# Query weights stored in the order in which they are loaded: runs of 16 KB per partition in place of 2 KB

## The reference

```python
def peer(h, w_query, sub_keys, expert_u, expert_v):      # h: 256 x 2048, in blocks of 128 tokens
    def block(xb):
        q = (xb @ w_query).reshape(128, 8, 2, 128)       # w_query: 2048 x 2048, 16.8 MB
        s = jnp.einsum('thpd,hpnd->thpn', q, sub_keys)   # scores against 2 x 128 keys for each head
        sv, si = lax.top_k(s, 16)
        ...                                              # 16 x 16 candidates, their best 16
        gate = jax.nn.softmax(top_s)
        act = jax.nn.gelu(jnp.einsum('thkd,td->thk', expert_u[idx], xb))
        return jnp.einsum('thk,thkd->td', gate * act, expert_v[idx])
```

## Time and profile before

| what | value |
|---|---|
| median of three runs | 1866.18 us |
| the profiled execution, device time | 1864.87 us |
| its span in the trace | 1863.2 us |
| PE busy | 1593.6 us (86%) |
| DVE busy | 1050.5 us (56%) |
| DMA packets, bytes | 73442, 724.64 MB, mean 389 GB/s |
| queue q0 (POOL) | 53472 packets, 613.75 MB, 78.8% of 16 engines |
| queue q1 (SP) | 17264 packets, 107.30 MB, 14.1% of 16 engines |

### The profile page before, as it was taken

The page is one execution under the profiler, slowest core; times in us unless marked ns, Lnnn a source line. Parts: engine busy times, 40 slices in busy tenths (PEclk is TensorE's granted clock), DMA queues, the critical chain, the costliest instruction groups (busy, mean ns, idle before and its releaser), DMA issues. The chain is left out here.

```text
span 1863.2 us, 13323 instructions
## 1 busy us (share of the span) xinstructions
PE 1593.6 (86%) x4518; PEld 761.0 (41%) x4518; DVE 1050.5 (56%) x1706; ACT 397.9 (21%) x1168; POOL 438.0 (24%) x384
## 2 busy tenths in 40 slices
PE   6999999999999979999877886877759687687776
PEld 2355445565458854443333332333324233232332
DVE  2237775675558873433546556465665656646445
ACT  2121013222010023222212222221223212122112
POOL 0000000001005565556322222221213122121212
PEclk9999999999999989999999999999889898999999
DMA  9998866548978999999999999999999999999997
GB/s 401 427 376 351 336 256 247 214 186 348 421 276 346 418 422 422 421 421 421 425 428 427 428 428 427 428 428 428 428 427 415 428 429 428 428 427 428 428 428 303
DMA packets 73442, 724.64 MB, mean 389 GB/s; under 512 B 7432, under 2 KB 9816, under 8 KB 20000
## 3 DMA queue, kind: packets, MB, share of 16 engines
q0 software_dynamic: 53472, 613.75, 78.8%
q1 hardware_dynamic: 17264, 107.30, 14.1%
q10 hardware_dynamic: 2640, 2.75, 0.5%
HBM read 721.63 MB, written 2.15 MB: 388 GB/s over the span
## 5 line engine op out<-in xcount | busy, mean ns | idle before, releaser
L1318 PE MATMUL ps<-ring,wg 128*128 128x512 f32 x1168 | 541.0, 613 | 130.5 <-ACT wg L851 111.0
L1766 DVE SCALAR_TENSOR_TENSOR ring<-ring,A 128x2048 f32<-128x2048 f32 x142 | 324.6, 2291 | 307.3 <-DMA ring<-in_expert_rows,acc 223.1
L1318 PEld LDWEIGHTS ps<-ring,wg 128*128 128x128 f32 x1168 | 221.8, 195 | 444.6 <-issue 275.8
L1023 PE MATMUL ps<-ring,H 128*128 128x512 f32 x512 | 222.1, 593 | 2.2 <-ACT rows_and_values L655 2.1
L513 POOL DMA_INDIRECT ring<-in_expert_rows,acc x106 | 116.1, 1095 | 388.7 <-PE ps L1318 376.5
L846 ACT ACTIVATE rows_and_values<-rows_and_values 128x1 f32<-128x1 f32 x256 | 50.9, 199 | 704.6 <-DVE ring L1766 398.4
L1318 PE MATMUL ps<-H,wg 128*128 128x512 f32 x360 | 167.3, 612 | 30.1 <-ACT wg L851 29.4
L1345 DVE SCALAR_TENSOR_TENSOR ring<-ring,rows_and_values 128x2048 f32<-128x2048 f32 x64 | 143.7, 2287 | 49.2 <-DMA ring<-in_mod_late 36.2
L1318 PE MATMUL ps<-rows_and_values,wg 128*128 128x512 f32 x288 | 135.5, 614 | 36.6 <-ACT wg L851 35.9
L1023 PEld LDWEIGHTS ps<-ring,H 128*128 128x128 f32 x512 | 96.4, 190 | 122.0 <-issue 118.9
L851 ACT ACTIVATE wg<-K,rows_and_values 128x128 f32<-128x128 f32 x256 | 102.7, 401 | 161.3 <-PE ps L1318 154.7
(11 more groups left out here) (281 smaller groups left out, 1464.4 us busy)
## 6 DMA issues: line engine op xcount, KB each, us to landing
ring<-in_mod_late POOLq DMA_DIRECT2D x32, 2048.0 KB, 10.5
ring<-in_mod_first SPq DMA_DIRECT2D x16, 2048.0 KB, 20.6
ring<-in_w_in SPq DMA_DIRECT2D x14, 2048.0 KB, 11.4
ring<-in_w_query SPq DMA_DIRECT2D x7, 2048.0 KB, 14.6
ring<-in_w_out SPq DMA_DIRECT2D x12, 1024.0 KB, 10.1
H<-in_tokens SPq DMA_DIRECT2D x4, 1024.0 KB, 13.0
queries_and_gates<-in_w_in SPq DMA_DIRECT2D x2, 1024.0 KB, 23.9
queries_and_gates<-neg_rows ACTq DMA_DIRECT2D x8, 256.0 KB, 5.2
```

Of the source, the lines that this page charges most:

```text
L1023: ins = mm(bank, H[:, kk, b * P:(b + 1) * P], W[kh][:, k, :], **flags)
L1318: ins = mm(ps[:, 4 * b + n, :], diag[:, r % 4, :], row[:, n * CH:(n + 1) * CH], start=k == 0, stop=r == BLOCK_RANKS - 1, skip_group_check= ...
L1766: v.scalar_tensor_tensor(out=rows_u, in0=rows_u, scalar=1.0, in1=A[:, r // BLOCK_RANKS, :], op0=ALU.mult, op1=ALU.mult, accum_out=dots[:, ...
```

## The change

The host lays out `w_query` with `pieces`, as it does `w_in` and `w_out`, so that its array is [4 blocks of columns, 2 halves, 128 partitions, 4096]. The two load functions read it in that shape. The bytes that land in each tile are the same, in the same places; the number, the order and the waits of the loads are the same. What differs is the run that lies together in HBM: 16 KB for each partition in a 2 MB piece (128 runs in place of 1024), and 8 KB in the two split pieces of 1 MB (128 in place of 512).

```diff
-        "w_out": pieces(w_out[0]), "w_query": w_query[0],
+        "w_out": pieces(w_out[0]), "w_query": pieces(w_query[0]),
...
             def load_third_query(kh, i, loaded):
-                k0 = (kh * KH + 4 * i) * P
-                sp.dma_start(WQ2[kh][i], w_query[k0:k0 + 4 * P, 2 * CH:3 * CH].rearrange(
-                    "(k p) n -> p k n", p=P)).then_inc(loaded, 16)
+                k0 = 4 * i * CH
+                sp.dma_start(WQ2[kh][i], w_query[2, kh, :, k0:k0 + 4 * CH].rearrange(
+                    "p (k n) -> p k n", k=4)).then_inc(loaded, 16)

             def load_query(n, kh):
                 base, loaded = (2, q_ld) if n % 2 == 0 else (0, w_ld)
-                sp.dma_start(W[base + kh], w_query[kh * KH * P:(kh + 1) * KH * P, n * CH:(n + 1) * CH
-                                                   ].rearrange("(k p) n -> p k n", p=P)).then_inc(loaded[kh], 16)
+                sp.dma_start(W[base + kh], w_query[n, kh].rearrange("p (k n) -> p k n", k=KH)
+                             ).then_inc(loaded[kh], 16)
```

## The result

The changed kernel took 1872.05 us, the median of seven runs (1870.87 to 1872.76), against 1866.18 for seven runs of the kernel before (1864.85 to 1866.84). The ratio is 1.0034, with a 95% interval of 1.0024 to 1.0043. The forecast was 1868.9, with a range up to 1871.4: the sign came out as worked out, the size did not, and a loss of over 0.2% had been given a chance of 0.28.

A forecast was written before the change was run, and what follows sets the result against it. DMA, filled by expert-row gathers from 700 to 1840 us, was taken as the bound. Row U 22 landing 2.7 us late gave 1864.87 + 2.7 = 1867.6 profiled, 1868.9 against the median 1866.18; 8-in-10 range 1864.4 to 1871.4.

The forecast's parts named there:

- Who gets the engines: Late query loads beside gathers: packets alternate one to one, so a 2 MB load takes 7.4 us in place of 25.
- part 2: Engine sharing at 578 to 682 us: long loads pass ahead of rows U, the third through at 618.0 us.
- The lateness of dot 15: Row U 15 late by 2.11 MB, 4.9 us, less 2 x 0.53 saved on two loads: 3.9 us.
- The empty DMA: During the pick of group 2, no query packets are left: DMA idle 3 to 5 us, near 636 to 640 us.
- My bounds: Landing of row U 22: 1.8 us late as U 0 on an empty DMA, 3.9 with 9.4 us again; 2.7 taken.
- the sum: Whole kernel: 1864.87 us profiled + 2.7 = 1867.6; against the median 1866.18, 1868.9.
- From U 22 to the end: Rows behind U 22 follow at the pace of the DMA; all 2.7 us reach V 0 and PE, nothing made up.
- The four slots starve: Rival before dot 15: more issues start under running dots, DMA empties, 2.1 us on top, 1871.0; chance 0.20.
- Sharing stays as it is: Rival: 16 KB runs served in smaller turns, dot 15 comes 1.1 us early, 1865.1 or 1864.6; chance 0.14.
- all of the saving counts: Rival: PE or the first gather hangs on the early loads, 4.3 us off, 1861.9; chance 0.05.
- The lateness is absorbed: Rival: part of the third load stays behind row U 15 and fills the lull, 1866.2 to 1867.5; chance 0.13.
- That a gain would be capped: At row V 0, issued behind PE's last scores: no more than 2.3 us can be gained.

The follow-up runs named there:

- late_2k: The changed kernel with the three query loads issued near 578, 595 and 609 us back in runs of 2 KB; 0.9995 of the kernel before.
- padded_2k: The changed kernel's layout with a gap of 256 bytes behind each 2 KB, so each packet is 2 KB again; 0.9999 of the kernel before.
- first_2k: The changed kernel with only the first late query load (near 578 us) back in runs of 2 KB; 1.0027 of the kernel before.
- late_16k: The kernel before with only the three late query loads in runs of 16 KB, the five early pieces in 2 KB; 1.0025 of it.
- second_16k: The changed kernel with the first and third late query loads back in 2 KB, only the middle one in 16 KB; 1.0014 of the kernel before.
- wait_dot15: The changed kernel with the last two query loads (n = 3) issued only after dot 15; 1.002 of the kernel before.
- third_16k: The changed kernel with the first two late query loads back in 2 KB, only the last (near 609 us) in 16 KB; 1.0005 of the kernel before.
- short_late: The kernel before with the three late query loads bringing only 128 of their 1024 rows, 5.5 MB left out; 0.9995 of it.
- third_waits: The changed kernel with only the last query load (n = 3, kh = 0) issued after dot 15; 1.0015 of the kernel before.

## Why the prediction was wrong in size, step by step

**Who gets the engines: right.** The packets alternate also at 16 KB (108 to 103 in 599 to 605 us). The third load was through at 620.9 us, 11.8 us after its issue: part 2 worked out 9.5 (2.1 + 7.4), but its first packet came 3.4 us after the issue in place of 2.1, and it moved for 8.4 us. It was still ahead of row U 15. late_2k and padded_2k show that neither the early loads nor the place in HBM takes part.

**The lateness of dot 15: 3.9 us worked out, 6.25 measured. This is the first step that failed.** The 2.11 MB that now come ahead are 5.0 us at 425 GB/s, as worked out. What was wrong is the term that I took off, 1.06 us saved on the first two loads. Counted from the empty DMA at 556 us to the same place behind dot 0, the kernel before (556 to 617.3 us) and the changed one (556 to 617.92 us) had moved:

```profile
DMA packets 4382, 21.08 MB, mean 344 GB/s; under 512 B 278, under 2 KB 278, under 8 KB 2322
```

```profile
DMA packets 2442, 20.95 MB, mean 338 GB/s; under 512 B 256, under 2 KB 256, under 8 KB 256
```

So nothing was won by then, and 0.13 MB, 0.3 us, were lost: what the longer packets saved went into the DMA left partly empty at 592 to 598 us, where the four slots starve (first_2k fills this stretch again). In late_16k, which has the same three long loads, the stretch is full (416 GB/s) and dot 15 is 4.97 us late, so not every execution pays this part. By the bytes row U 15 is then 3.9 + 1.06 + 0.3 = 5.3 us late.

The last 1.0 us is in how the row lands. The trace keeps sixteen landings for each transfer, which I take for one of each DMA engine, and the dot waits for the last of them. In the kernel before they came at 617.58 to 617.93 us, in the changed one at 623.03 to 624.81; their middle (617.69 and 623.48 us) is 5.2 us late behind dot 0, as the bytes have it, and the last 6.3. That the engines drift apart does not come from long packets: the sixteen landings of this row are 1.9 us apart in late_2k and 2.3 in padded_2k, and under 1.1 only in the kernel before and in second_16k. So 1.0 of the 6.25 us may belong to the two executions and not to the change.

**The empty DMA: right in place, and its price follows from the lateness.** U 22 was issued 6.0 us late, onto an empty DMA, and landed 7.3 us after its issue: at 646.15, 3.9 us late. My bounds from a lateness of 3.9 were 1.8 to 3.9; with 6.0 in its place the lower one, as for U 0, reads 3.9. So the term of 2.7 us in the sum measured 3.9. These are the issues of U 15, U 22 and U 37 in the changed kernel, us to landing:

```profile
gy<-in_expert_u,acc POOLq DMA_INDIRECT x1, 11.3
...
ring<-in_expert_u,acc POOLq DMA_INDIRECT x1, 7.3
...
ring<-in_expert_u,acc POOLq DMA_INDIRECT x1, 11.4
```

**From U 22 to the end: put at nothing, measured 1.2 us to V 0 and some 0.5 behind it. This is the second step that failed.** U 37 landed at 673.88 + 11.4 = 685.3 us, 5.06 us late, and V 0 with it. The 1.2 us between U 22 and U 37 is DMA lost after the empty stretch (at 650 to 652 us it moved 266 GB/s, in the kernel before 426). I had put all rows behind U 22 at the pace of the DMA. But up to the one at 660.62 us the dots follow each other without a wait, and each gather is issued behind a dot, so there is no queue of rows that could cover a gap; this is read from the order of time and not tested. From V 0 to the first store another 0.5 us are added, which no run here explains, and 0.3 us are the difference between the profiled executions and the medians: 3.9 + 1.2 + 0.5 + 0.3 = 5.9 us, where the sum had 2.7.

**The rivals.** "The four slots starve" had its mechanism: issues under a running dot took 2 to 3 us, and wait_dot15 shows the starving by itself. I gave it 0.20 as an alternative; it came on top of the forecast, as the bunching that I forecast would bring it about. Its time, 1871.0, came nearest, but by luck in part: its 2.1 us were the price of one held issue, and what was measured at the two places before U 22 is 0.9 us each over the kernel before (592 to 598 and 618 to 630 us). "Sharing stays as it is" and "all of the saving counts" are out (late_16k, late_2k). "The lateness is absorbed" is what third_16k does on purpose.

**That a gain would be capped: right.** short_late leaves out 14 us of transfers, and PE starts 2.33 us earlier, where the prediction allowed 2.3. At the first store 1.15 us of it are left, and of the median 0.8 us, within its interval.

## What to carry to other kernels

In this kernel the time that longer packets save would count only on a DMA that is full anyway; beside another queue they also buy a larger share of the engines, so a transfer that nobody waits for should keep its packets short while one that somebody waits for is in flight. Before making a background load faster, look in its window for stretches where it alone moved: if the queue that matters leaves gaps there, the load was free, and once it is gone early the gaps stand empty. A lateness handed to an engine that works in a fixed order is to be followed through the long step behind it, up to the first transfer that waits for a buffer.

## What the runs showed of the hardware

- One packet was one run of the layout at all sizes tried, and two queues that both had work moved as many packets each: 535 to 531 with 8 KB rows against runs of 2 KB in the kernel before, and 103 to 108 with 8 KB rows against runs of 16 KB in the changed one, where the loads had 1.72 MB to 0.81 in 6 us.
- Runs of 2 KB moved at 386 GB/s, of 8 KB at 422 and of 16 KB at 428.
- POOL's issue of an indirect DMA took 0.94 us when DVE was between dots, and 1.9 to 3.0 when it started under a dot, ending 0.8 to 0.9 us after that dot.
- The sixteen landings of one gathered row of 1 MB lay 0.35 us apart in the kernel before, 1.78 in the changed one and 3.46 in third_waits; the dot started behind the last of them.
